# Narrow weight blocks in two products, and a front whose modulation, turning and splitting of tokens run side by side

## The reference

```python
mod_lat = silu(c) @ w_ada + b_ada            # and mod_ctx from c_ctx
shift, scale, gate = split(mod_lat, 3)
hm = rmsnorm(h, norm_w) * (1 + scale) + shift   # h: x (2048 rows), ctx (256 rows)
p = hm @ w_in                                # 1024 x 5152; its last 32 columns are dt
...
dt = softplus(p[..., OFF_DT:] + dt_bias)     # 32 columns
...
p2 = h2 @ w_in_2                             # second block; its last 8 columns are the forget gates
```

## Time and profile before

| | us |
|---|---|
| median of 3 runs (lowest, highest) | 3491.55 (3487.11, 3496.17) |
| the profiled execution | 3487.76 |
| its span, first to last instruction | 3486.1 |
| PE busy | 3263.6 (94%) |
| DVE busy | 1637.1 (47%) |
| ACT busy | 967.4 (28%) |
| POOL busy | 384.9 (11%) |

### The profile page before, as it was taken

The page is one execution under the profiler, slowest core; times in us unless marked ns, Lnnn a source line. Parts: engine busy times, 40 slices in busy tenths (PEclk is TensorE's granted clock), DMA queues, the critical chain, the costliest instruction groups (busy, mean ns, idle before and its releaser), DMA issues. The chain is left out here.

```text
span 3486.1 us, 37796 instructions
## 1 busy us (share of the span) xinstructions
PE 3263.6 (94%) x15012; PEld 2561.4 (73%) x15012; DVE 1637.1 (47%) x1886; ACT 967.4 (28%) x1798; POOL 384.9 (11%) x246
## 2 busy tenths in 40 slices
PE   7899999997999979996999979999998799999898
PEld 7688888876887857774888867878877455555577
DVE  2754443466014237875444434323424455555365
...
PEclk9999999999999968887999989999999699999899
...
GB/s 160 72 79 60 96 88 119 121 151 85 71 101 200 129 145 155 154 145 151 119 111 113 122 104 126 92 95 93 73 84 66 106 61 42 57 48 7 79 130 106
DMA packets 210926, 358.43 MB, mean 103 GB/s; under 512 B 22030, under 2 KB 143502, under 8 KB 202899
## 3 DMA queue, kind: packets, MB, share of 16 engines
...
...
## 5 line engine op out<-in xcount | busy, mean ns | idle before, releaser
L636 PE MATMUL p_ps<-hmT_hi,p_w_hi 128*128 128x512 f32 x1312 | 524.4, 400 | 21.5 <-ACT p_work L356 15.9
L636 PE MATMUL p_ps<-hmT_hi,p_w_lo 128*128 128x512 f32 x1312 | 513.6, 391 | 0.0
L636 PE MATMUL p_ps<-hmT_lo,p_w_hi 128*128 128x512 f32 x1312 | 513.1, 391 | 0.0
L1751 PE MATMUL p_ps<-h2T_hi,p_w_hi 128*128 128x512 f32 x800 | 328.1, 410 | 19.3 <-DVE h2T_lo L1610 19.3
L1751 PE MATMUL p_ps<-h2T_hi,p_w_lo 128*128 128x512 f32 x800 | 316.1, 395 | 0.0
L1751 PE MATMUL p_ps<-h2T_lo,p_w_hi 128*128 128x512 f32 x800 | 315.8, 395 | 0.0
L636 PEld LDWEIGHTS p_ps<-hmT_hi,p_w_hi 128*128 128x128 f32 x1312 | 248.1, 189 | 75.5 <-issue 21.1
L636 PEld LDWEIGHTS p_ps<-hmT_hi,p_w_lo 128*128 128x128 f32 x1312 | 247.7, 189 | 53.1
L636 PEld LDWEIGHTS p_ps<-hmT_lo,p_w_hi 128*128 128x128 f32 x1312 | 248.2, 189 | 49.3
L1913 PE MATMUL t_psO<-t_prob,t_v 128*65 128x512 f32 (+3 forms) x640 | 261.0, 530 | 0.9 <-DVE t_out_turned L2023 0.2
L1970 ACT ACTIVATE t_prob<-t_psS 128x1024 f32<-128x1024 f32 (+1 forms) x160 | 150.2, 938 | 307.7 <-PE t_psS L1901 178.1
...
## 6 DMA issues: line engine op xcount, KB each, us to landing
p_w_raw<-in_w_in SPq DMA_DIRECT2D x66, 512.0 KB, 6.1
p_spare<-in_wada ACTq DMA_DIRECT2D x32, 512.0 KB, 5.5
p_spare<-scratch_xs_tok SPq DMA_DIRECT2D x19, 512.0 KB, 4.4
...
p_work<-in_wada SPq DMA_DIRECT2D x16, 512.0 KB, 3.5
p_work<-in_x SPq DMA_DIRECT2D x16, 512.0 KB, 3.3
...
```

The source lines that it names most:

```text
L636: mm = pe.matmul(PS[:, c, 0:width], wt[n][:, q, :], xx[:, q, cols], start=(q == 0 and j == 0), stop=(q == KT - 1 and j == 2))
L1751: mm = pe.matmul(ps[:, c, :], wt[n][:, q, :], xx[:, q, c * CH:(c + 1) * CH], start=(q == 0 and j == 0), stop=(q == KT - 1 and j == 2))
```

## The change

In `front`:

- The modulation blocks come in pairs, the shift and the scale of one feature tile `q` behind each other, and each pair writes a bank of its own (banks 0 to 3, `mod_bank`). VectorE computes `mS` and `mA` of tile `q` as soon as its pair is there (`modulation(q)`).
- `turn_x(j - 3)` follows each modulation block from j = 3 on, so that 13 of the 18 tiles are turned between them. The turned tile is copied out of PSUM unmodulated (`turned_out`: one 512-column instruction on ScalarE, one on VectorE) into a float32 buffer `normT` that lies where `hmT_lo` will be.
- Modulating and splitting are done in 40 pieces (chunk `c`, feature tile `q`), in an order written out as `PIECES_AT`: ScalarE writes the high part of 512 columns, VectorE computes the same in float32 into `temp` and subtracts. GpSimd no longer takes part.
- Block 0 is multiplied in half chunks, each waiting for its pieces, with the last five tiles turned between them. There are three `xt` buffers in place of two.
- Block `DT` puts the low part of its 32 real columns in columns 32 to 63 of `w_hi`; the product then takes two matmuls per tile, not three, and VectorE adds the two halves after turning (`dt_sum`).

In `projection2` the same is done for block 0 with the low part in columns 32 to 39; two rows of `flT` are stored and loaded, and added in `forget`.

```diff
-xt, xn, full = ([work[:, (2 * m + n) * D:(2 * m + n + 1) * D] for n in range(2)] for m in range(3))
+xt, xn = ([work[:, (m + n) * D:(m + n + 1) * D] for n in range(cnt)] for m, cnt in ((0, 3), (3, 2)))
+temp = [work[:, 5 * D + n * CH:5 * D + (n + 1) * CH] for n in range(2)]
+xTc = spare[:, KT * CTX:2 * KT * CTX].rearrange("p (k n) -> p k n", n=CTX)
+PIECES_AT = {5: ((0, 0), (0, 1)), 6: ((0, 2),), 7: ((0, 3),), 8: ((0, 4),), 9: ((1, 0), (1, 1)), 10: ((1, 2), (1, 3), (0, 5)),
+             11: ((1, 4), (1, 5)), 12: ((0, 6), (1, 6)), 13: ((2, 0), (2, 1), (2, 2)),
+             14: ((0, 7), (1, 7), (2, 3)), 15: ((2, 4), (2, 5)), 16: ((2, 6), (2, 7)), 17: ((3, 0), (3, 1)),
+             18: ((3, 2), (3, 3)), 19: tuple((3, q) for q in range(4, KT)) + tuple((4, q) for q in range(KT))}
+PIECES = [p for n in sorted(PIECES_AT) for p in PIECES_AT[n]]
+mod_bank = lambda q: PS[:, q % 4, 0:8].rearrange("p (m c) -> p m c", c=4)
...
+def turned_to(t, half):
+    part = slice(half * 4, half * 4 + 4)
+    return xT[:, part, t * P:(t + 1) * P] if t < LT else xTc[:, part, (t - LT) * P:(t - LT + 1) * P]
+def piece_of(c, q):
+    cols = chunk_cols(c)[0]
+    return (xT[:, q, cols], hm_hi[:, q, cols], hm_lo[:, q, cols]) if c < NCH else \
+        (xTc[:, q, :], hc_hi[:, q, :], hc_lo[:, q, :])
 turn_bank = lambda n: (PS[:, 5, :], PS[:, 6, :]) if n == 0 else (PS[:, 7, :], PS[:, 4, :])
...
-    sp.dma_start(wb[j % 3], a["wada"][j]).then_inc(a_in[j % 3], 16)
+    sp.dma_start(wb[j % 3], a["wada"][j // 2 + KT * (j % 2)]).then_inc(a_in[j % 3], 16)
 def load_x(t):
-    if t >= 2:
-        sp.wait_ge(S["xn"], t - 1)
-    sp.dma_start(xt[t % 2], a["x"][t * P:(t + 1) * P, :] if t < LT
-                 else a["ctx"][(t - LT) * P:(t - LT + 1) * P, :]).then_inc(x_in[t % 2], 16)
+    if t >= 3:
+        sp.wait_ge(S["xn"], t - 2)
+    sp.dma_start(xt[t % 3], a["x"][t * P:(t + 1) * P, :] if t < LT
+                 else a["ctx"][(t - LT) * P:(t - LT + 1) * P, :]).then_inc(x_in[t % 3], 16)
...
 if b == DT:
+    sp.wait_ge(S["dt_sum"], 1)
...
 for j in range(3, 16):
     load_ada(j)
-    if j == 6:
-        load_x(2)
-    if j == 8:
-        load_x(3)
-    if j in (10, 12):
-        load_w(j // 2 - 5)
-for t in range(4, TT):
+    load_x(j - 1)
+    if j in (10, 13):
+        load_w(0 if j == 10 else 1)
+for t in range(15, TT):
...
-def affine(t):
-    n, which = t % 2, 0 if t < LT else 1
+def turned_out(t):
     act.wait_ge(S["turned_x"], t + 1)
-    if t >= 2:
-        act.wait_ge(S["lo"], t - 1)
-    for q in range(4):
-        ins = act.activation(tiles(full[n])[:, q, :], tiles(turn_bank(n)[0])[:, q, :], ACT.Identity,
-                             scale=mA[:, which, q:q + 1], bias=mS[:, which, q:q + 1])
-    ins.then_inc(S["full_a"], 1)
+    act.activation(turned_to(t, 0), tiles(turn_bank(t % 2)[0]), ACT.Copy).then_inc(S["out_a"], 1)
+def piece(c, q):
+    which = 0 if c < NCH else 1
+    act.wait_ge(S["out_a"], min(4 * c + 4, TT))
+    act.wait_ge(S["out_v"], min(4 * c + 4, TT))
+    act.wait_ge(S["mod"], q + 1)
+    x, hi, lo = piece_of(c, q)
+    act.activation(hi, x, ACT.Identity, scale=mA[:, which, q:q + 1], bias=mS[:, which, q:q + 1]).then_inc(S["hi"], 1)
...
-for t in range(3):
-    norm(t)
-act.wait_ge(S["mod"], 2)
-for t in range(TT):
-    affine(t)
-    if t + 3 < TT:
-        norm(t + 3)
-    if t < 2:
-        high(t)
+for t in range(TT + 2):
+    if t < TT:
+        norm(t)
+    if t >= 2:
+        turned_out(t - 2)
+    for c, q in PIECES_AT.get(t, ()):
+        piece(c, q)
+    if t == 12:
+        high(0)
+    if t == 18:
+        high(1)
...
-for t in range(TT):
-    g.wait_ge(S["full_a"], t + 1)
-    g.wait_ge(S["full_v"], t + 1)
-    dst = hm_hi[:, :, t * P:(t + 1) * P] if t < LT else hc_hi[:, :, (t - LT) * P:(t - LT + 1) * P]
-    g.tensor_copy(dst, tiles(full[t % 2])).then_inc(S["hi"], 1)
...
-def affine(t):
-    n, which = t % 2, 0 if t < LT else 1
+    v.tensor_scalar(xn[n], xt[t % 3], stat[:, 2, n:n + 1], None, ALU.mult).then_inc(S["xn"], 1)
+def turned_out(t):
     v.wait_ge(S["turned_x"], t + 1)
-    if t >= 2:
-        v.wait_ge(S["hi"], t - 1)
-    for q in range(4):
-        ins = v.tensor_scalar(tiles(full[n])[:, 4 + q, :], tiles(turn_bank(n)[1])[:, q, :], mA[:, which, 4 + q:5 + q],
-                              mS[:, which, 4 + q:5 + q], ALU.mult, ALU.add)
-    ins.then_inc(S["full_v"], 1)
-def low_x(t):
-    v.wait_ge(S["hi"], t + 1)
-    hi, lo, at = (hm_hi, hm_lo, t) if t < LT else (hc_hi, hc_lo, t - LT)
-    cols = slice(at * P, (at + 1) * P)
-    v.tensor_tensor(lo[:, :, cols], tiles(full[t % 2]), hi[:, :, cols].bitcast(F32),
-                    ALU.subtract).then_inc(S["lo"], 1)
+    v.tensor_copy(turned_to(t, 1), tiles(turn_bank(t % 2)[1])).then_inc(S["out_v"], 1)
+def modulation(q):
+    v.wait_ge(S["mod_used"], 2 * q + 2)
+    v.tensor_scalar(mS[:, :, q], mod_bank(q)[:, 0, 0:2], s.cols1[:, V_BADA + q:V_BADA + q + 1], None, ALU.add)
+    v.tensor_scalar(mA[:, 0:2, q], mod_bank(q)[:, 1, 0:2], mA[:, 2, q:q + 1], s.cols1[:, V_NORM + q:V_NORM + q + 1],
+                    ALU.add, ALU.mult).then_inc(S["mod"], 1)
+def piece(c, q):
+    m, which = PIECES.index((c, q)), 0 if c < NCH else 1
+    v.wait_ge(S["out_a"], min(4 * c + 4, TT))
+    v.wait_ge(S["out_v"], min(4 * c + 4, TT))
+    v.wait_ge(S["mod"], q + 1)
+    if m >= 2:
+        v.wait_ge(S["lo"], m - 1)
+    x, hi, lo = piece_of(c, q)
+    full = temp[m % 2][:, 0:chunk_cols(c)[1]]
+    step(v.tensor_scalar(full, x, mA[:, which, q:q + 1], mS[:, which, q:q + 1], ALU.mult, ALU.add))
+    v.wait_ge(S["hi"], m + 1)
+    v.tensor_tensor(lo, full, hi.bitcast(F32), ALU.subtract).then_inc(S["lo"], 1)
 def low(b):
     v.wait_ge(S["w_hi"], b + 1)
     if b >= 2:
         v.wait_ge(S["chunk"], chunks_before(b - 1))
-    v.tensor_tensor(w_lo[b % 2][:], w_raw[b % 2][:], w_hi[b % 2][:].bitcast(F32),
-                    ALU.subtract).then_inc(S["w_lo"], 1)
+    if b == DT:
+        own = w_raw[b % 2][:, :, 0:NDH], w_hi[b % 2][:, :, 0:NDH].bitcast(F32)
+        v.tensor_tensor(w_hi[b % 2][:, :, NDH:2 * NDH], *own, ALU.subtract).then_inc(S["w_lo"], 1)
...
+if b == DT and gs[-1] == 4:
+    v.wait_ge(S["group_read"], groups_before(DT + 1))
+    v.tensor_tensor(tok[:, 0:TT, 0:NDH], tok[:, 0:TT, 0:NDH], tok[:, 0:TT, NDH:2 * NDH],
+                    ALU.add).then_inc(S["dt_sum"], 1)
...
-for t in range(3):
-    if t == 2:
-        v.wait_ge(S["turned_x"], 1)
-    xnorm(t)
-v.wait_ge(S["mod_used"], 16)
-for w in range(2):
-    v.tensor_tensor(mS[:, w, :], psC[:, 0:KT, w], s.cols1[:, V_BADA:V_BADA + KT], ALU.add)
-    step(v.tensor_tensor(mA[:, w, :], psC[:, KT:2 * KT, w], s.cols1[:, V_BADA + KT:V_BADA + 2 * KT], ALU.add))
-    v.scalar_tensor_tensor(mA[:, w, :], mA[:, w, :], 1.0, s.cols1[:, V_NORM:V_NORM + KT],
-                           ALU.add, ALU.mult).then_inc(S["mod"], 1)
-v.wait_ge(S["mod"], 2)
-for t in range(TT):
-    affine(t)
-    if t + 3 < TT:
-        v.wait_ge(S["turned_x"], t + 2)
-        xnorm(t + 3)
-    if t < 2:
-        low(t)
-    low_x(t)
-v.wait_ge(S["lo"], TT)
+step(v.tensor_scalar(mA[:, 2, :], s.cols1[:, V_BADA + KT:V_BADA + 2 * KT], 1.0, None, ALU.add))
+for t in range(TT + 2):
+    if t < TT:
+        xnorm(t)
+    if t >= 2:
+        turned_out(t - 2)
+    if t % 2 == 0 and t < 2 * KT:
+        modulation(t // 2)
+    for c, q in PIECES_AT.get(t, ()):
+        piece(c, q)
+    if t == 12:
+        low(0)
+    if t == 18:
+        low(1)
+v.wait_ge(S["lo"], len(PIECES))
...
+def mod_first(j):
+    pe.wait_ge(a_in[j % 3], 16 * (j // 3 + 1))
+    for q in range(KT):
+        mm = pe.matmul(mod_bank(j // 2)[:, j % 2, 0:3], wb[j % 3][:, q, :], sc3[:, q, :], start=(q == 0), stop=(q == KT - 1))
+    mm.then_inc(S["mod_used"], 1)
...
-pe.wait_ge(S["full_a"], t - 1)
-pe.wait_ge(S["full_v"], t - 1)
+pe.wait_ge(S["out_a"], t - 1)
+pe.wait_ge(S["out_v"], t - 1)
...
-for j, (wt, xx) in enumerate(((w_hi, hi), (w_hi, lo), (w_lo, hi))):
+if b == 0:
+    pe.wait_ge(S["lo"], PIECES.index((c, q)) + 1)
+terms = ((w_hi, hi), (w_hi, lo)) + (((w_lo, hi),) if b != DT else ())
+for j, (wt, xx) in enumerate(terms):
     mm = pe.matmul(PS[:, c, 0:width], wt[n][:, q, :], xx[:, q, cols],
-                   start=(q == 0 and j == 0), stop=(q == KT - 1 and j == 2))
+                   start=(q == 0 and j == 0), stop=(q == KT - 1 and j == len(terms) - 1))
...
-    mod_cols(j, a_in, wb, psC).then_inc(S["mod_used"], 1)
-    if j == 9:
-        turn_x(0)
-    if j == 11:
-        turn_x(1)
-for t in range(2, 6):
-    turn_x(t)
+    if j % 2 == 0 and j >= 8:
+        pe.wait_ge(S["mod"], j // 2 - 3)
+    mod_first(j)
+    if j >= 3:
+        turn_x(j - 3)
 pe.wait_ge(S["w_lo"], 1)
-for t in range(6, TT):
-    c, part = (t - 6) // 4, (t - 6) % 4
-    if part == 0:
-        pe.wait_ge(S["lo"], 4 * c + 4)
-    product(0, c, (2 * part, 2 * part + 1))
-    turn_x(t)
-pe.wait_ge(S["lo"], LT)
-product(0, 3, range(KT))
-pe.wait_ge(S["lo"], TT)
-product(0, 4, range(KT))
+for c in range(5):
```

(31 more changed lines are left out.)

37 lines of the change are left out of this document (22 added, 15 removed).

## The result

The changed kernel took 3448.7 us (median of four runs, 3437.8 to 3452.0) where the kernel before took 3489.3 us in the same session: 40.6 us less, ratio 0.9877 with a 95% interval of 0.9855 to 0.9899. The forecast was 34.6 us less. The profiled execution has a span of 3449.3 us against 3486.1.

A forecast was written before the change was run, and what follows sets the result against it. Front was taken as PE bound, then DVE bound, and blocks 1 to 40 as PE bound. Gains of 24.6 + 8.2 + 1.8 = 34.6 us took the 3491.6 us median to 3457 us, range 3443 to 3472.

The forecast's parts named there:

- What bounds the kernel: Front is PE bound with DVE idle, then DVE bound; blocks 1 to 40 are bound by PE.
- part 1: Front's first stage: 16 modulation blocks and 13 tiles take PE 77.3 us, to 85.5 us, with no waits.
- Parts 2 and 3: Front's token loop and tail: pieces cost DVE 1.19 us; block 1 starts at 122.0 us, 24.6 us gained.
- Part 4: First projection's block 16: two thirds of its 24.6 us remain, 8.2 us gained, with its evacuations covered.
- Part 5: Second projection's block 0: only chunk 3 gets shorter, by 1.8 us; a 3 us loss if PE's clock falls.
- Rival 1: Front: the clock rises during the modulation; block 1 at 93 us, the kernel at 3428 us; chance 5%.
- Rival 2: Front: pieces cost about 2 us through hand-overs; block 1 at 145 us, the kernel at 3480 us; chance 12%.
- rival 3: Front: slower, since pieces cost over 2.5 us; at 2.8 us each the kernel takes 3503 us; chance 3%.
- Rival 4: Block 16 gains nothing because the convolution's chain is later than read; the kernel at 3465 us; chance 4%.

The follow-up runs named there:

- doubled pieces: The changed kernel with the tensor_scalar of every piece issued twice on DVE; 3453.9 us.
- the run with short copies: The changed kernel with 160 GpSimd copies of 220 float32 columns beside the token loop, into an unread buffer; 3458.7 us.
- single fillers: The changed kernel with one extra 256-column matmul of ones behind each modulation product, into an unread bank; ratio 0.9954.
- two fillers: The changed kernel with two extra 256-column matmuls of ones behind each modulation product, into an unread bank; 3454.6 us, ratio 0.9922.

## Why the prediction was right

**What bounds the kernel, and part 1.** The reading of two stages one behind the other holds: DVE's work slid beneath a PE that stayed full. No load and no `xn` made PE wait. The term was mis-sized by 1.3 us in PE's favour: the period is 5.01 us, not 3.41 + 1.75 = 5.16. A tile costs 1.74 us, as read; a block behind a tile costs 27.27 - 24.00 = 3.27 us, and 3.41 is the cost behind another block. `turn_x(12)` was done at 84.4 us, not 85.7.

**Parts 2 and 3.** A piece costs 1.18 us (forecast 1.19) and a context piece 0.79 (0.8); the line through two durations of other lengths and the start-to-start times of neighbours gave both. What failed is the sentence that the surplus of iterations 10 to 13 stays under 1 us. At iteration 12 DVE still waited; iterations 12 and 13 took 5.85 and 5.54 us (75.94, 81.79, 87.33) against PE's 5.01, and put it 1.4 us behind. From 78.85 us on it was busy almost without a gap, with waits of 0.28 to 0.36 us for ACT's high part where ACT had itself waited for `mod_scale` or for DVE's copy of a turned tile. So the 1.3 us that PE won were not used: `xnorm(14)` started at 87.33 where the forecast had 87.4, for another reason. Iteration 14 then took 5.9 us, not 5.4, and iteration 15 began at 93.2 where the forecast had it wait for `turn_x(13)` until 93.5; that tile was turned from 88.5 us on, not from 90.7. From there the list ran as written: iteration 18 at 105.2 (105.2), DVE done at 121.1 (121.1), block 1 at 122.00 (122.0). The agreement to 0.1 us is partly luck, errors of half a microsecond to more than one against each other. The clock did not fall at the end, as assumed. With doubled pieces it did: a short product takes 0.21 us there in place of 0.12, and block 1 begins at the slow pace, its second and third matmul 0.42 us apart.

A piece's `tensor_tensor` takes 0.69 us, and 0.61 to the next start; by the line through 0.69 us at 512 and 1.22 at 1024 columns some 0.16 us of it are fixed (an estimate), so about half of the fixed part is overlapped, a little less than the "most of it" of the prediction. That is the trace's word on the fixed cost per instruction of "VectorE: DVE Perf Modes", section "The TRN2 errata", in the Trainium skill. With the exclusive lock of "SBUF — State Buffer", section "SBUF: two separate sides", in the Trainium skill, the rows of before and the run with short copies agree: the price is the rest of GpSimd's instruction, not a constant.

**Part 4** is right to 0.1 us, and its cover held: behind `silu(15)` ACT evacuated three chunks of block 16 from 527.29 us on, 4.5 us ahead of the last one at 531.79, and PE did not wait.

**Part 5** has its mechanism right (chunk 3 still starts when the last `low_h` is done, 2.97 us of waiting in place of 0.16) and its 1.8 us too (8.16 to 6.30 us; 6.30 to 6.35 in nine of the ten profiles with the narrow block, 8.12 to 8.29 in those without). The tenth, with single fillers, took 7.85 us: behind the same pause of 2.97 us PE came back at the slow pace there, 0.43 us apart, and the granted clock was 0.50 for 3 us. That is the loss that the prediction had named as possible; it came once. But "only chunk 3 itself gets shorter" was wrong: 500 us later the same stage gave 6 to 9 us more. No row of before showed this, and its cause is still open. It can account for the 6.0 us by which the measured 40.6 exceed the 34.6, and for most of the 11.8 us of the 46.4; the scatter of the third stretch is as large.

**The range.** Of its bounds only the shorter pieces pull the time down, by 3 us, to 3454. No term of the prediction leads to its 3449. The measured 3448.7 us lie in the range of 3443 to 3472 by the allowance for the spread of the runs, and what brought the time there is in the main the stretch that had no term.

**The rivals.** Rival 1, the clock rising during the modulation, did not come; PE did its 3-column products and one tile per block for 75 us at the slow pace. The kernel with two fillers shows that the clock can rise there. Rival 2 fell with 1.18 us per piece, and rival 3 with it; the doubled pieces (1.76 us) show what it would have done, block 1 at 138.4. Rival 4 did not come.
